# Key/value compression contracted over 128 partitions, compressed probabilities padded to 32 columns

## The reference

```python
# k_c, v_c: [tokens, 2 kv heads, 64]; blocks of 32 tokens, one every 16: n_cmp = 15
blocks = t[:, :, tok] + pos                               # [2 heads, 15, 32, 64]
kc = blocks.reshape(B, G, n_cmp, 32 * 64) @ w             # w: [2048, 64], one for k, one for v
p_c = masked_softmax(einsum('bgrqd,bgnd->bgrqn', qb, kc), m_c)   # 8 query heads, 15 columns
o_c = einsum('bgrqn,bgnd->bgrqd', p_c, vc)
out = gate0 * o_c + gate1 * o_s + gate2 * o_w
```

## Time and profile before

| | |
|---|---|
| median of 3 runs | 1282.09 us (1279.1 to 1283.16) |
| span of the profiled execution | 1278.0 us |
| TensorE, matmuls | 1144.9 us busy (90%) |
| VectorE | 860.1 us (67%) |
| ScalarE | 311.8 us (24%) |
| GpSimd | 329.6 us (26%) |
| mean granted TensorE clock | 0.993 |

### The profile page before, as it was taken

One profiled execution on the slowest core, in us unless ns is written; L12 is line 12 of the kernel. 1 busy time (PEld: TensorE's weight loads), 2 busy tenths in 40 slices (PEclk: granted clock), 3 DMA queues, 4 the chain that ended last, 5 costly groups with the idle time before them and its releaser, 6 DMA issues.

```text
span 1278.0 us, 14904 instructions
## 1 busy us (share of the span) xinstructions
PE 1144.9 (90%) x5224; PEld 702.7 (55%) x5224; DVE 860.1 (67%) x2305; ACT 311.8 (24%) x1005; POOL 329.6 (26%) x285
## 2 busy tenths in 40 slices
PE   8999999999999999999999989899786877777777
PEld 5876758767855677887656444445232323222222
DVE  2747735375545687873788777778778777777655
ACT  0125300234211133330232222222222222222222
POOL 0000000000001000000334544556644544545430
PEclk9999999999999999999999999999999999999999
DMA  8771156842343567533899999999999999999995
GB/s 335 312 264 67 67 197 225 298 170 87 121 197 136 211 213 265 206 145 129 347 425 424 422 424 425 423 425 424 423 422 424 424 423 423 423 424 424 422 424 208
DMA packets 54826, 391.27 MB, mean 306 GB/s; under 512 B 8120, under 2 KB 10680, under 8 KB 15840
## 3 DMA queue, kind: packets, MB, share of 16 engines
q0 software_dynamic: 37792, 269.63, 50.8%
q1 hardware_dynamic: 16960, 120.68, 25.1%
HBM read 389.22 MB, written 1.07 MB: 305 GB/s over the span
## 4 chain that ended last, share of the span: by engine, by line
PE 51%; DMA 35%; DVE 10%; ACT 2%; issue 2%; POOL 0%; SPq 0%; DVEq 0%; ACTq 0%
PE bank L548 15%; DMA arena<-peer_uv_in,arena 14%; PE bank L542 13%; PE bank L1123 9%; DMA wring<-peer_uv_in,arena 9%; DMA const<-peer_uv_in,arena 5%; DMA hT<-peer_uv_in,arena 5%; PE bank L954 2%; PE bank L1034 2%; DMA wring<-w_in 2%; PE bank L577 2%; DVE arena L1592 2%; PE bank L614 1%; PE bank L600 1%; PE bank L770 1%
## 5 line engine op out<-in xcount | busy, mean ns | idle before, releaser
L1123 PE MATMUL bank<-arena 128*128 128x512 f32 x464 | 220.3, 609 | 50.4 <-ACT arena L1559 50.1
L548 PE MATMUL bank<-hT,wring 128*128 128x256 f32 (+1 forms) x1344 | 245.0, 341 | 1.3 <-ACT arena L1345 0.8
L548 PEld LDWEIGHTS bank<-hT,wring 128*128 128x128 f32 x1344 | 216.3, 191 | 35.0 <-issue 13.5
L1123 PE MATMUL bank<-wring,arena 128*128 128x512 f32 x336 | 160.2, 612 | 37.0 <-ACT arena L1559 35.3
L2413 POOL DMA_INDIRECT arena<-peer_uv_in,arena x114 | 139.3, 1222 | 164.0 <-PE bank L1123 140.4
L2308 DVE CUSTOM_DVE_ANT_0 arena<-arena 128x1024 f32<-128x1024 f32 x116 | 141.5, 1222 | 55.6 <-DMA arena<-peer_uv_in,arena 55.3
L1123 PEld LDWEIGHTS bank<-arena 128*128 128x128 f32 x464 | 84.6, 192 | 167.6 <-issue 87.5
L2378 POOL TENSOR_TENSOR small<-small,const 128x1 f32<-128x1 f32 (+3 forms) x18 | 16.1, 897 | 576.7 <-DVEq L1604 260.9
L1123 PEld LDWEIGHTS bank<-wring,arena 128*128 128x128 f32 x336 | 61.9, 193 | 124.5 <-issue 65.8
L2308 DVE CUSTOM_DVE_ANT_0 wring<-wring,arena 128x1024 f32<-128x1024 f32 x84 | 102.5, 1222 | 41.3 <-DMA wring<-peer_uv_in,arena 39.3
L2413 POOL DMA_INDIRECT wring<-peer_uv_in,arena x84 | 99.2, 1181 | 92.1 <-PE bank L1123 83.9
(11 more groups left out here) (238 smaller groups left out, 1347.0 us busy)
## 6 DMA issues: line engine op xcount, KB each, us to landing
wring<-w_in SPq DMA_DIRECT2D x22, 2048.0 KB, 10.0
wring<-ada_in SPq DMA_DIRECT2D x12, 2048.0 KB, 8.3
wring<-wo_in SPq DMA_DIRECT2D x5, 2048.0 KB, 7.8
wring<-cmp_in SPq DMA_DIRECT2D x2, 2048.0 KB, 7.7
wring<-br_in SPq DMA_DIRECT2D x2, 2048.0 KB, 8.6
arena<-pq_in SPq DMA_DIRECT2D x2, 2048.0 KB, 9.8
wring<-pq_in SPq DMA_DIRECT2D x2, 2048.0 KB, 9.1
wring<-w1b_in SPq DMA_DIRECT2D x2, 1120.0 KB, 7.4
```

What stands on the lines that cost most here:

```text
L548: ins = pe.matmul(bank[:, at:at + n_tok], w[:, k, col:col + P], rhs[:, k, :], start=(k == 0), stop=(k == KC - 1))
L1123: ins = pe.matmul(sums_of[half][:, :], diag[:, at % NDIAG, :], v_row[slot_of[at]][:, half * 512:(half + 1) * 512], start=(n == 0), stop=(n ...
```

## The change

Three things are done in each layer.

First, the blocks are laid out with the early 16 offsets in partitions 0 to 63 and the late 16 in partitions 64 to 127, both heads side by side in the columns (`key_blocks`, `value_blocks`). VectorE writes them with eight instructions of 64 partitions and 240 columns. The weight chunk `cmp` is reordered to match and is 1 MB instead of 2 MB, since it is no longer held twice. TensorE contracts in 16 steps over 128 partitions, for both heads at once: 16 matmuls for keys (64 weight columns, 30 moving) and 16 for values (64 weight columns, the heads padded to 32 each, 64 moving). The values of the two heads land in partitions 0 to 14 and 32 to 46.

Second, the compressed probabilities are padded to 32 columns for each head (`cmp_pad`) and ordered so that four heads fill 128 columns. A transpose takes four heads; there are 4 in a layer instead of 16, in 2 banks instead of 4.

Third, the round's compressed part reads `vc` and `cmpT` from partitions 0 to 14 for head 0 and from 32 to 46 for head 1.

```diff
-        blocksT = take(2 * CMP_L * CMP_N).rearrange("p (b l n) -> p b l n", b=2, l=CMP_L)
+        key_blocks = take(2 * CMP_L * CMP_N)[:, 0:CMP_L * CMP_N].rearrange("p (l g n) -> p l g n", l=CMP_S, g=2)
-        cmp_s = take(TT * 8 * CMP_N).rearrange("p (t h n) -> p t h n", t=TT, h=8)
+        cmp_pad = take(TT * 8 * CMP_P).rearrange("p (t h n) -> p t h n", t=TT, h=8)
+        cmp_s = cmp_pad[:, :, :, 0:CMP_N]
-        cmpT = take(TT * 8 * P).rearrange("p (t h s) -> p t h s", t=TT, h=8)
+        cmpT = take(TT * 4 * P).rearrange("p (t a o s) -> p t a o s", t=TT, a=2, o=2)
+        value_pad = take(CMP_S * 2 * CMP_P).rearrange("p (l c) -> p l c", l=CMP_S)
+        value_blocks = value_pad.rearrange("p l (g n) -> p l g n", g=2)[:, :, :, 0:CMP_N]
...
-                for l in range(CMP_L):
-                    for g in range(2):
-                        r = slice(g * HD, (g + 1) * HD)
-                        ins = pe.matmul(bank[r, 0:CMP_N], w[r, 0, l, :], blocksT[r, 0, l, :],
-                                        start=(l == 0), stop=(l == CMP_L - 1))
+                for l in range(CMP_S):
+                    ins = pe.matmul(bank[0:HD, 0:2 * CMP_N], w[:, 0, l, :], key_blocks[:, l, :, :],
+                                    start=(l == 0), stop=(l == CMP_S - 1))
                 finish(ins, ("kc", L))
-                vc_bank = [job(("vc", L, g)) for g in range(2)]
-                for l in range(CMP_L):
-                    for g in range(2):
-                        r = slice(g * HD, (g + 1) * HD)
-                        ins = pe.matmul(vc_bank[g][0:CMP_N, 0:HD], blocksT[r, 1, l, :], w[r, 1, l, :],
-                                        start=(l == 0), stop=(l == CMP_L - 1))
+                bank = job(("vc", L))
+                for l in range(CMP_S):
+                    ins = pe.matmul(bank[0:2 * CMP_P, 0:HD], value_pad[:, l, :], w[:, 1, l, :], start=(l == 0), stop=(l == CMP_S - 1))
...
-                                v, weight = vc[0:CMP_N, half], cmpT[0:CMP_N, t, 4 * g + r, :]
+                                n_of = slice(CMP_P * g, CMP_P * g + CMP_N)
+                                v, weight = vc[n_of, :], cmpT[n_of, t, r // 2, r % 2, :]
...
-                    for half in range(2):
-                        bank = job(("cT", L, t, half))
-                        for j in range(4):
-                            ins = pe.transpose(bank[0:CMP_N, j * P:(j + 1) * P], cmp_s[:, t, 4 * half + j, :], ident)
-                        finish(ins, ("cT", L, t, half))
+                    transposes(("cT", L, t), [cmp_pad[:, t, 4 * a:4 * a + 4, :].rearrange("p h n -> p (h n)") for a in range(2)])
...
-                free(copy(kcT, bank[:, 0:CMP_N]), ("kc", L))
-                for g in range(2):
-                    bank = full(act, ("vc", L, g))
-                    free(copy(vc[0:CMP_N, g * HD:(g + 1) * HD], bank[0:CMP_N, 0:HD]), ("vc", L, g))
+                copy(kcT[0:HD, :], bank[0:HD, 0:CMP_N])
+                free(copy(kcT[HD:P, :], bank[0:HD, CMP_N:2 * CMP_N]), ("kc", L))
+                bank = full(act, ("vc", L))
+                free(copy(vc[0:2 * CMP_P, :], bank[0:2 * CMP_P, 0:HD]), ("vc", L))
...
+            dve.memset(cmp_pad, 0.0)
+            dve.memset(value_pad, 0.0)
...
-                for b in range(2):
-                    ins = tt(blocksT[:, b, :, :], view(bank[:, :], b * S, [[1, CMP_L], [CMP_S, CMP_N]]),
-                             every(par[:, V_POS + (L * 2 + b) * CMP_L:V_POS + (L * 2 + b + 1) * CMP_L], CMP_N, 2), ALU.add)
+                for late in range(2):
+                    to = slice(late * HD, (late + 1) * HD)
+                    for g in range(2):
+                        r = slice(g * HD, (g + 1) * HD)
+                        for b in range(2):
+                            at = V_POS + (L * 2 + b) * CMP_L + late * CMP_S
+                            ins = tt((key_blocks, value_blocks)[b][to, :, g, :], view(bank[r, :], b * S + late * CMP_S, [[1, CMP_S], [CMP_S, CMP_N]]),
+                                     every(par[r, at:at + CMP_S], CMP_N, 2), ALU.add)
```

More of the change, by code:

```diff
@@ L35 @@
 CMP_S = 16
+CMP_P = 32
 LRU_C = 8.0
@@ L245, in program @@
         ret_s = probs.rearrange("p j c -> p (j c)")[:, 0:3 * 512].rearrange("p (j c) -> p j c", j=3)
-        cmp_s = take(TT * 8 * CMP_N).rearrange("p (t h n) -> p t h n", t=TT, h=8)
+        cmp_pad = take(TT * 8 * CMP_P).rearrange("p (t h n) -> p t h n", t=TT, h=8)
+        cmp_s = cmp_pad[:, :, :, 0:CMP_N]
         probsT = take(2 * D).rearrange("p (j c) -> p j c", j=2)
-        cmpT = take(TT * 8 * P).rearrange("p (t h s) -> p t h s", t=TT, h=8)
+        cmpT = take(TT * 4 * P).rearrange("p (t a o s) -> p t a o s", t=TT, a=2, o=2)
+        value_pad = take(CMP_S * 2 * CMP_P).rearrange("p (l c) -> p l c", l=CMP_S)
+        value_blocks = value_pad.rearrange("p l (g n) -> p l g n", g=2)[:, :, :, 0:CMP_N]
         kcT = take(CMP_N)
-        vc = take(P)
+        vc = take(HD)
         y = take(TT * S).rearrange("p (t c) -> p t c", t=TT)
@@ L486, in width @@
         def width(chunk):
+            if chunk[0] == "cmp":
+                return 2 * CMP_S * HD
             if chunk[0] == "w1" and chunk[2] == 4:
@@ L669, in _ @@
                 w_used(("w1", L, 4), ("vg", L, 1))
-                w = weights(("cmp", L, 0)).rearrange("p (b l e) -> p b l e", b=2, l=CMP_L)
+                w = weights(("cmp", L, 0)).rearrange("p (b l e) -> p b l e", b=2, l=CMP_S)
                 taken(pe, ("kcvc", L))
                 bank = job(("kc", L))
-                for l in range(CMP_L):
-                    for g in range(2):
-                        r = slice(g * HD, (g + 1) * HD)
-                        ins = pe.matmul(bank[r, 0:CMP_N], w[r, 0, l, :], blocksT[r, 0, l, :],
-                                        start=(l == 0), stop=(l == CMP_L - 1))
-                finish(ins, ("kc", L))
-                vc_bank = [job(("vc", L, g)) for g in range(2)]
-                for l in range(CMP_L):
-                    for g in range(2):
-                        r = slice(g * HD, (g + 1) * HD)
-                        ins = pe.matmul(vc_bank[g][0:CMP_N, 0:HD], blocksT[r, 1, l, :], w[r, 1, l, :],
-                                        start=(l == 0), stop=(l == CMP_L - 1))
-                        if l == CMP_L - 1:
-                            finish(ins, ("vc", L, g))
-                w_used(("cmp", L, 0), ("vc", L, 1))
+                for l in range(CMP_S):
+                    ins = pe.matmul(bank[0:HD, 0:2 * CMP_N], w[:, 0, l, :], key_blocks[:, l, :, :],
+                                    start=(l == 0), stop=(l == CMP_S - 1))
+                finish(ins, ("kc", L))
+                bank = job(("vc", L))
+                for l in range(CMP_S):
+                    ins = pe.matmul(bank[0:2 * CMP_P, 0:HD], value_pad[:, l, :], w[:, 1, l, :], start=(l == 0), stop=(l == CMP_S - 1))
+                finish(ins, ("vc", L))
+                w_used(("cmp", L, 0), ("vc", L))
                 w = weights(("w1", L, 5)).rearrange("p (k c) -> p k c", k=KC)
@@ L797, in _ @@
                     pe.wait_ge(sem("cmp_scaled"), TT * L + t + 1)
-                    for half in range(2):
-                        bank = job(("cT", L, t, half))
-                        for j in range(4):
-                            ins = pe.transpose(bank[0:CMP_N, j * P:(j + 1) * P], cmp_s[:, t, 4 * half + j, :], ident)
-                        finish(ins, ("cT", L, t, half))
+                    transposes(("cT", L, t), [cmp_pad[:, t, 4 * a:4 * a + 4, :].rearrange("p h n -> p (h n)") for a in range(2)])
                 gate_columns_t(0)
-                for g in range(2):
-                    taken(pe, ("vc", L, g))
+                taken(pe, ("vc", L))
                 for t in range(TT):
                     taken(pe, ("vg", L, t))
-                    for half in range(2):
-                        taken(pe, ("cT", L, t, half))
+                    taken(pe, ("cT", L, t))
                 for p in range(len(rounds)):
@@ L1366, in _ @@
                 for t in range(TT):
[L1367 to L1370, removed]
+                    bank = full(act, ("cT", L, t))
+                    for odd in range(2):
+                        ins = copy(cmpT[0:2 * CMP_P, t, :, odd, :],
+                                   bank[odd * HD:(odd + 1) * HD, 0:2 * P].rearrange("p (a s) -> p a s", a=2))
+                    free(ins, ("cT", L, t))
                 gate_tanh(0)
@@ L1789, in _ @@
                         bank = full(dve, ("nc", L, t, g))
-                        free(tt(cmp_s[:, t, 4 * g:4 * g + 4, :], bank[:, 0:4 * CMP_N].rearrange("p (h n) -> p h n", h=4),
+                        free(tt(cmp_s[:, t, g::2, :], bank[:, 0:4 * CMP_N].rearrange("p (h n) -> p h n", h=4),
                                 every(cm, 4), ALU.add), ("nc", L, t, g))
@@ L1807, in _ @@
                     link(dve.reciprocal(coef_c, sums[:, t, :, 0]))
-                    link(tt(coef_c, coef_c, gates3[:, t, :, 0], ALU.mult))
```

(6 more changed lines are left out.)

## The result

The changed kernel takes 1273.95 us (median of 4 runs, 1272.48 to 1274.88), the kernel before 1281.89 us in the same comparison (1279.1 to 1283.16). The ratio is 0.9936, with a 95% interval of 0.9921 to 0.9952: 6 to 10 us faster. Forecast were 1274.2 us and a gain of 7.9.

The account below looks back on a forecast made before the run. TensorE was taken to bound the compression stage, VectorE's loop the pace at the transposes. Products 4.10 less wait 0.9 plus transposes 0.4, and 4.28 in layer 1, made 7.9 us: 1282.1 to 1274.2 us, range 1272 to 1277.

Parts of the forecast that it names:

- Products: Compression matmuls on TensorE: 3.84 us a layer, saving 4.10 us in layer 0 and 4.28 us in layer 1.
- the serial rival: Weight loads do not overlap running matmuls: compression matmuls take 6.2 us a layer, total 1278.1 us; chance 0.08.
- The wait in layer 0: TensorE waits 0.9 us for weight load `w1 5` before `rvg 0`; bounds 0 and 2.8 us.
- a sign of being wrong: A wait over 2 us for weight load `w1 5` would make the prediction wrong.
- the blocks: VectorE's eight block instructions take 2.64 us instead of 1.22, plus 1.42 us, moving the issue of `w1 5` to 69.4.
- The sum: Whole kernel: 3.6 us gained in layer 0 plus 4.28 in layer 1, 7.9 us, giving 1274.2 us on the median.
- Layer 1: No wait for `w1 5` (bounds 0 and 1.9 us), nothing from the transposes; 4.28 us gained.
- Transposes: 12 fewer a layer: 2.6 us of TensorE time, on the path 0.4 us in layer 0 and 0 in layer 1.
- The slower one: Rounds: the array empties between the heads' 32-partition groups, plus 0.73 us a round, 11.7 us in all, 1285.9 us; chance 0.04.
- Late weights: VectorE's blocks plus 2.2 us, landings as long as before: waits of 2.9 and 1.9 us, 1278.1 us; chance 0.12.

Follow-up runs that it names:

- the products alone: The changed kernel with only the products contracted over 128 partitions, probabilities transposed one head at a time as before: 1273.06 us, ratio 0.9938 to the kernel before.
- the transposes alone: The kernel before with only the compressed probabilities padded and transposed four heads at a time, products still 64 partitions deep: 1282.6 us, ratio 1.0005.

## Why the prediction was right

**Products: right, with a starting point that was a little long.** 3.84 us a layer forecast, 3.87 to 3.88 measured where no wait follows, and no pause in them: each record, with 64 weight columns against 30 or 64 moving ones, takes about 0.06 us. A weight load hides behind the running matmul at full depth, so the serial rival (6.2 us) is out. What the prediction took for that rival from the Trainium skill (TensorE: Matmul & The Clock Gate, "The mechanism"), that a weight load overlaps running matmuls only when the row groups differ, does not hold for these full-depth float32 passes, as it did not for the transposes. Against the first profile the change in TensorE's pace is 4.1 and 4.2 us, forecast 4.10 and 4.28. Against all executions of the kernel before without a fall in the stage (means 7.69 and 7.82 us) it is 3.8 and 3.9.

**The wait in layer 0: right in kind, too small.** Forecast 0.9 us; measured 1.41, 1.36 with the products alone, and 2.51 in the first profile, which is over the 2 us that the prediction had named as a sign of being wrong. Its terms: the blocks cost 1.72 us more (2.94 against 1.22), not 1.42; the load took 7.2 to 7.5 us, not 8.0; and VectorE began the blocks at 57.4 to 58.4 us, not 57.07, which the prediction had taken as fixed. That start hangs on an input load and moves between executions; in those with the old products it lay at 56.93 to 57.88. Moving the blocks (no wait, 2.3 us off the median) shows that this path was the bound.

**The clock: missed on both sides.** No term of the prediction had it. In the first profile after, it cost 1.7 us behind the wait, so that layer 0 gained nothing where 3.2 were forecast. In the second, it fell at 132 us instead, and the round there took 4.05 us (131.81 to 135.86) where it had taken 3.36 (134.49 to 137.85). Against it stand the falls inside the 64-deep products, which cost the kernel before 3.0 us in the one of five executions that had one.

**The sum: partly luck.** The forecast of 7.9 us was set on the median, which stood 4.1 us above the first span. Only 1.9 of these lie around the span, and the prediction did not ask what the other 2.2 were. Without a fall in its products the kernel before reaches the first gather at 615.3 to 616.7 us, the changed kernel in its two profiles at 611.9 and 610.4: a gain of 3.4 to 6.3 us. The second of these took 1273.81 us, nearly the median, and against the mean of the four before (616.0) it gained 5.6. The rest of the measured 7.9, some 2.3 us, is by this working what falls in the products add to the median execution of the kernel before. That is an estimate: most of the timed runs have no profile. So the places of the change gave some 2 us less than forecast (products 0.6, wait 0.5, transposes 0.4, the slower round 0.7), and the end of a loss that nobody had counted made up for it.

**Layer 1: right.** No wait, as forecast; 4.24 us against the first profile. Some 0.3 us are given back in the rounds, where the clock fell at 284 us: the gate columns behind the scores of 294.74 start 4.38 us earlier, at 292.37 instead of 296.75, where `rvg 0` had started 4.69 earlier.

**Transposes: forecast 0.4 us, nothing seen.** The medians cannot show 0.4 us, but the traces come near. From the start of `rvg 0` in layer 0 to the first gather, less the products of layer 1, the transposes alone take 527.7 us, and the five executions of the kernel before take 527.5 to 528.0. The gate columns start 105.08 instead of 107.18, 1.85 us earlier against the products' shift of 0.25, exactly as computed, and VectorE's 0.42 us wait is gone. But 10 us later VectorE pauses 0.58 us where it paused 0.21 before, and at 137 us the shift is again that of 87 us. With the transposes alone this pause stayed at 0.21 us; its cause is open, since the trace names VectorE itself as the releaser. In layer 1 the forecast of nothing held.

**Rivals.** The slower one (head 1 in another 32-partition group) is out: a round's first 12 value records take 1.02 to 1.03 us before and after, where that rival wanted 0.73 us more:

```profile
115.45 1.03 PE L771 MATMUL bank<-arena 15*64 15x128 f32 x12
```

Late weights were half right: the blocks and their start were late, which moved the release of the slot by 2.2 to 3.2 us instead of 1.4, but the landing was short and layer 1 had no wait.

What stays open: that the grouped transposes bring the falls at 130 and 280 us is a count of 6 to 0, not a mechanism. TensorE has less to do there (35.2 us busy of the 40 from 100 to 140, 36.7 before), but no run changed that alone.

## What to carry to other kernels

When a stage on the bound engine gets shorter, look for whoever then comes last: here the release of a weight slot by VectorE, behind which instructions had been placed that the change made longer. Moving eight instructions behind the release gave back what the wait took. And one profile is one execution: where its time stands apart from the median, find out what the other executions do at the places of the change before that distance enters a forecast.

## What the runs showed of the hardware

A pass of a float32 matmul took as long as the larger of weight columns and moving columns wanted, at about 0.9 ns a column, whether 64 or 128 partitions deep: 64 and 30, and 64 and 64, both took about 0.06 us (64 records in 3.88 us). The granted clock fell to one half while TensorE was busy in every microsecond, in streams of 64-deep matmuls with 15 columns on one side (6.8 us of 10.69 in layer 1 at 1282.25 us). Four other executions of the same code showed no such fall in either layer.
